# Dilated attention with its values made in a stage of their own: six projection blocks per head instead of nine, queries in reversed order

## The chip, the cores and the metric

The kernel runs on one core of one Trainium2 chip. The metric is the device time of one execution in microseconds (us). Each kernel has several runs, of which the median is given, and one further execution that the hardware profiler recorded. All views of the profile below come from that one recorded execution.

The engines of a core work side by side and meet at semaphores: TensorE (PE; its loads of the stationary operand are listed apart as PEld), VectorE (DVE), ScalarE (ACT), GpSimd (POOL) and SyncE (SP), which here only issues DMAs. Each engine takes its own instructions strictly in the order in which they are written.

## The reference, cut to what matters

The model has a first block (forgetful attention, retention, memory attention) and a second block. The change is in the dilated attention of the second block: three groups of four heads; head j of all three groups is joined by the weights of their softmax denominators.

```python
DILATED_PATTERNS = ((128, 1), (512, 4), (2048, 16))     # window, dilation of a group
h = rms_norm(x, norm_mix_pre)
q, k, v, glu_in, gates = split(h @ w_in)                # 512 positions, 12 heads of 128
for g, (window, r) in enumerate(DILATED_PATTERNS):      # heads 4g .. 4g+3
    # query t sees the keys t - j*r, j = 0 .. window//r
    s = q @ k.T * Dh**-0.5 + bias[bucket(distance)]     # masked outside the window
    m = max(s); p = exp(s - m); l = sum(p)
    o = (p @ v) / l
w = l * exp(m - max over groups of m)                   # joined over the groups
a = sum(w * o) / sum(w)
y_a = a @ w_attn_out
c = silu(layer_norm(causal_conv(glu(glu_in), 31 taps))) # beside it
y_c = c @ conv_pw_w
mixed = sigmoid(gates_a) * y_a + sigmoid(gates_c) * y_c
```

## The kernel before

**Projections.** Activations lie with channels on the partitions and 512 positions along the row, as a high and a low part (`Hh`, `Hl`). Weights come in blocks of 512 KB from DRAM (`wraw`, issued by SP, line 515), ACT rounds them to a high part (`whi`, helper `split`, line 755), POOL makes the low part (`wlo`, line 600), and PE multiplies them with the activations in 24 matmuls of 512 columns per block (`products`, lines 2190 to 2192: high by high, high by low, low by high). The blocks go round a ring of four places. The DMA of block n is issued when PE has finished block n-4; ACT's `split` call that stands at block b of its program handles block b+3, POOL's handles block b+2. So a weight block that lands late first blocks ACT, with all that stands behind the `split` in ACT's program.

**The dilated stage ("dil").** For each of the four heads j, nine blocks in the order of `DIL_BLOCKS`: q and k of group 0, of group 1, of group 2, then v of the three groups. DVE takes each result out of PSUM and scales it by the row norm: q to `dq`, k to `dk` in reversed order of positions (lines 1950, 1953), v to `dvT` (line 1956). For groups 1 and 2 the positions are read by residue mod 4. As the value operand must have positions on the partitions, PE turns `dvT` by four transposes per group (`d_values`, line 2646) and ACT copies the result to `dv` (`d_vtok`, line 1136): 12 times in all.

A head's softmax goes over two layouts: lay 0 (group 0, tiles of 128 consecutive positions) and lay 1 (groups 1 and 2, by residue). The steps are: `d_score(h, lay)` on PE; `d_soft` on DVE (bias and row maximum, line 1856); `d_exp` on ACT (line 1094); `d_store` and `d_load` on ACT's DMA queue (lines 1102 and 1108), which carry the row maxima and sums through a small DRAM buffer from one layout to the other; `d_diffs` on DVE; `d_weights_of` on ACT (line 1113); `d_weigh` on DVE; `d_norm` on ACT (line 1121, eight instructions, which signal after four and after eight); `d_turn` on PE (15 transposes, line 2616); `d_copy` on ACT (line 1128); `d_weigh_band` and `d_weigh_residues` on PE (lines 2627, 2637); `d_result` on ACT and DVE. The last head has a small matmul (`d_swap`) in place of the trip through DRAM.

**What lies beside it.** DVE computes the convolution of 31 taps for 8 chunks as 248 instructions (`taps`, line 1817), some behind each evacuation. POOL sums the chunks (line 696) and their squares (line 702), and PE forms mean and variance from the sums; ACT and DVE then normalise the chunks (`layer_norm`, lines 1147 to 1168 and 1918 to 1926) during the last head. The order on each engine is written out by hand: `d_stage(h, b)` is ACT's list for block b of head h, and the loops at the end of each engine's program are those of DVE and PE. Where PE stands at a block, the step that needs another engine's result is placed some blocks later.

## Time and profile before

| | |
|---|---|
| median of 3 runs | 1819.2 us (1818.88 to 1819.79) |
| the profiled execution, its own time | 1818.85 us |
| its span in the profile | 1817.2 us |
| PE busy | 1809.6 us (100% of the span) |
| PEld, DVE, ACT, POOL busy | 83%, 50%, 42%, 43% |
| "dil" stage | from about 1010 us to about 1242 us of the span |

The busy time of PE is the union of its matmuls, whose recorded ends overlap. How fast PE really goes is read from the distance between the starts of successive instructions in the timeline. "Idle before" in a row is the time for which the engine stood still before the instruction, and the name behind the arrow is what ended that.

### The profile page before, as it was taken

Reading aid. Unit: us, or ns where it says so; the run is one execution under the profiler, and the core shown is the slowest. Engines: PE = TensorE matmul, PEld = TensorE weight load, DVE = VectorE, ACT = ScalarE, POOL = GpSimd, SP = SyncE. Lnnn points to the kernel's source line nnn. Section 1 sums busy time; section 2 is a strip of 40 time slices with the busy share of each in tenths; the row PEclk is TensorE's granted clock in tenths of the full one; section 3 lists DMA queues with packets and bytes.
Section 4 is the critical chain, followed back from the end, with each engine's and each line's share of the span. In section 5 each row is a group of like instructions: output and inputs, shape, how many; then the busy total and the mean of one; then the engine's idle time right before and its main releaser. Section 6 shows DMA issues by size and latency. Waiting matters only on the chain.

```text
span 1817.2 us, 23583 instructions
## 1 busy us (share of the span) xinstructions
PE 1809.6 (100%) x8529; PEld 1500.7 (83%) x8529; DVE 916.1 (50%) x1583; ACT 759.7 (42%) x1228; POOL 786.6 (43%) x380
## 2 busy tenths in 40 slices
PE   9999999999999999999999999999999999999998
PEld 7888888888888777888888888888888888888887
DVE  6246566454210565544249989866333564544202
ACT  5344344443233565543343233257223474444213
POOL 3544443443444333443444543353444454444442
PEclk9999999999999999999999999999999999999999
DMA  5333333323333323332333443322333333333332
GB/s 175 100 93 83 92 81 93 111 82 105 93 93 115 93 81 93 98 100 81 103 93 93 113 89 83 81 82 69 94 102 94 93 93 93 92 103 105 95 102 93
DMA packets 285751, 173.99 MB, mean 96 GB/s; under 512 B 14800, under 2 KB 271208, under 8 KB 285664
## 3 DMA queue, kind: packets, MB, share of 16 engines
q1 hardware_dynamic: 275264, 164.70, 31.6%
q0 software_dynamic: 2496, 8.07, 1.5%
q10 hardware_dynamic: 7904, 0.06, 0.2%
q8 instruction: 55, 0.90, 0.2%
q14 instruction: 32, 0.26, 0.1%
HBM read 170.62 MB, written 2.19 MB: 95 GB/s over the span
## 4 chain that ended last, share of the span: by engine, by line
PE 99%; DVE 0%; ACT 0%; DMA 0%; issue 0%; DVEq 0%; ACTq 0%
PE proj L2190 23%; PE proj L2192 23%; PE proj L2191 23%; PE A L2508 1%; PE A L2510 1%; PE A L2509 1%; PE A L2871 1%; PE A L2873 1%; PE A L2872 1%; PE A L2348 1%; PE A L2446 1%; PE PV L2446 1%; PE proj L2510 1%; PE proj L2509 1%; PE proj L2508 1%; PE A L2438 1%
## 5 line engine op out<-in xcount | busy, mean ns | idle before, releaser
L600 POOL TENSOR_TENSOR wlo<-wraw,whi 128x1024 fp32r<-128x1024 f32 (+1 forms) x304 | 721.2, 2376 | 922.0 <-ACT whi L755 917.2
L755 ACT ACTIVATE whi<-wraw 128x1024 fp32r<-128x1024 f32 (+1 forms) x303 | 317.7, 1050 | 626.4 <-DMA wraw<-w_in 159.5
L2190 PE MATMUL proj<-Hh,whi 128*128 128x512 f32 x1424 | 562.8, 395 | 0.0
L2192 PE MATMUL proj<-Hh,wlo 128*128 128x512 f32 x1424 | 555.2, 390 | 0.0
L2191 PE MATMUL proj<-Hl,whi 128*128 128x512 f32 x1424 | 554.7, 390 | 0.0
L2192 PEld LDWEIGHTS proj<-Hh,wlo 128*128 128x128 f32 x1424 | 267.2, 188 | 56.7
L2190 PEld LDWEIGHTS proj<-Hh,whi 128*128 128x128 f32 x1424 | 267.5, 188 | 54.8 <-issue 0.7
L2191 PEld LDWEIGHTS proj<-Hl,whi 128*128 128x128 f32 x1424 | 267.6, 188 | 54.2 <-issue 0.7
L1817 DVE SCALAR_TENSOR_TENSOR A<-cin,dwT,A 128x512 f32<-128x512 f32 x232 | 175.1, 755 | 6.8
L2190 PE MATMUL proj<-Oh,whi 128*128 128x512 f32 x256 | 99.8, 390 | 0.0
L2191 PE MATMUL proj<-Ol,whi 128*128 128x512 f32 x256 | 99.6, 389 | 0.0
L2192 PE MATMUL proj<-Oh,wlo 128*128 128x512 f32 x256 | 99.6, 389 | 0.0
L1732 DVE TENSOR_TENSOR X<-X,proj 128x512 f32 (+1 forms) x16 | 11.0, 688 | 93.9 <-PE proj L2192 93.9
L2192 PEld LDWEIGHTS proj<-Oh,wlo 128*128 128x128 f32 x256 | 48.0, 188 | 10.1
L2190 PEld LDWEIGHTS proj<-Oh,whi 128*128 128x128 f32 x256 | 48.1, 188 | 9.8
L2191 PEld LDWEIGHTS proj<-Ol,whi 128*128 128x128 f32 x256 | 48.1, 188 | 9.8
L2126 DVE TENSOR_TENSOR uv<-proj,rms 128x512 f32<-128x512 f32 x21 | 14.5, 692 | 81.3 <-PE proj L2192 81.3
L2164 DVE TENSOR_TENSOR VT<-VT,gains 128x512 f32<-128x512 f32 x1 | 0.7, 700 | 101.2 <-ACT sq L1395 101.2
L858 ACT ACTIVATE ztanh<-z 128x512 f32<-128x512 f32 x20 | 12.6, 632 | 72.2 <-DVE z L1612 43.1
L1989 DVE TENSOR_TENSOR sq<-proj,rms 128x512 f32<-128x512 f32 x16 | 11.0, 690 | 54.0 <-PE proj L2192 54.0
L2508 PE MATMUL A<-whi,Hh 128*128 128x512 f32 x96 | 37.8, 394 | 0.0
L1586 DVE SCALAR_TENSOR_TENSOR ob<-PV,gate 128x512 f32<-128x512 f32 x20 | 13.8, 691 | 47.1 <-PE PV L2371 25.7
(553 smaller groups left out, 2948.8 us busy)
## 6 DMA issues: line engine op xcount, KB each, us to landing
wraw<-w_in SPq DMA_DIRECT2D x68, 512.0 KB, 3.8
wraw<-fox_w_in SPq DMA_DIRECT2D x56, 512.0 KB, 3.8
wraw<-ret_w_in SPq DMA_DIRECT2D x44, 512.0 KB, 3.8
wraw<-w_up SPq DMA_DIRECT2D x44, 512.0 KB, 3.8
wraw<-w_out SPq DMA_DIRECT2D x40, 512.0 KB, 4.0
wraw<-w_down SPq DMA_DIRECT2D x22, 512.0 KB, 3.6
wraw<-w_mem_kv SPq DMA_DIRECT2D x16, 512.0 KB, 3.9
wraw<-conv_pw_w SPq DMA_DIRECT2D x8, 512.0 KB, 4.0
```

The lines of the kernel that those rows point to most:

```text
L600: pool.tensor_tensor(wlo[s][:, 0:r, :], wraw[s][:, 0:r, :], whi[s][:, 0:r, :].bitcast(F32), ALU.subtract).then_inc(w_lo, 1)
L755: f(whi[s][:, 0:r, :], wraw[s][:, 0:r, :], ACT.Copy).then_inc(w_hi, 1)
L1817: ins = stt(conv_sum if tap < CONV - 1 else C[:, c, :], cin[:, c, tap:tap + S], dwT[:, c * CONV + tap:c * CONV + tap + 1], conv_sum, ALU.m ...
L2190: mm(dst, whi[s][:, c, :], xh, start=(first and c == 0), stop=False)
L2191: mm(dst, whi[s][:, c, :], xl, start=False, stop=False)
L2192: ins = mm(dst, wlo[s][:, c, :], xh, start=False, stop=(last and c == chunks - 1))
L2348: ins = pe.transpose(A[j][:, (i - j) * P:(i - j + 1) * P], probs[:, FOXAT[i] + j * P:FOXAT[i] + (j + 1) * P], ident[:])
L2438: ins = mm(ret_place(e, j), k[rows, j * P:(j + 1) * P], q[rows, j * P:S], start=True, stop=True)
L2446: ins = mm(ret_sum[e][:, j * P:S], values[:, r, j * P:(j + 1) * P], decayed[e][:, TRI[j]:TRI[j] + S - j * P], start=(j == 0), stop=(j == N ...
L2508: mm(y, Hh[:, x, at], high[:, c, :], start=(x == 0), stop=False)
L2509: mm(y, Hl[:, x, at], high[:, c, :], start=False, stop=False)
L2510: ins = mm(y, Hh[:, x, at], low[:, c, :], start=False, stop=(x == KC - 1))
```

## The change

- The values of all heads of a group are made by a new stage "vd" between "glu" and "dil". Its twelve weight blocks (four per group, each 2 x 128 rows by 512 columns, which is the values of four heads) are the moving operand, and 128 positions of `Hh` or `Hl` are the stationary one, so the result has positions on the partitions at once. Again 24 matmuls per block (`dil_values`, new lines 2635 to 2637). For groups 1 and 2 the stationary operand is read by residue, every fourth element of the row (`tokens_of`). ACT takes the tiles out of PSUM and applies the row norm as a scale per partition (`keep_dil`, new line 1186, 12 instructions).
- That scale per partition, `d_roots`, comes from eight matmuls of one column (new line 2607), four of them with `rms` read by residue, and one DVE instruction.
- `d_values`, `d_vtok` and the evacuation to `dvT` are gone; a head has six blocks. The steps of its softmax are spread anew over six blocks: `d_score(h, 1)`, its exp, its store and both loads move to the first two blocks of the next head, `d_turn` behind its fourth and the weighing behind its fifth.
- Queries are stored in reversed order instead of keys, the result is read reversed, and the bias table is mirrored.
- 84 taps of the convolution move to the new stage, and the sums, the layer norm and the last head's steps are placed anew.

```diff
-DIL_BLOCKS = ((0, 0), (0, 1), (1, 0), (1, 1), (2, 0), (2, 1), (0, 2), (1, 2), (2, 2))
-CHUNK_SUMS = (0, 5, 10, 15, 21, 26, 29)
+TAPS_GLU, TAPS_VALUES = (6, 5), 84
+TAPS_DIL = ((6, 6, 6, 6, 4, 6), (4, 4, 6, 8, 8, 5), (4, 4, 6, KC * CONV, 0, 0), (0, 0, 0, 0, 0, 0))
+DIL_BLOCKS = ((0, 0), (0, 1), (1, 0), (1, 1), (2, 0), (2, 1))
+CHUNK_SUMS = (0, 4, 8, 13, 18, 23, 27)
+SQUARE_SUMS = {29: (1, 2, 3), 30: (4, 5), 31: (6, 7)}
+        def tokens_of(x, spread, t):
+            return residues(x)[:, t, :] if spread else x[:, t * P:(t + 1) * P]
 # ACT
+            def keep_dil(group):
+                for j in range(NT):
+                    if j < NT - 1:
+                        act.wait_ge(v_summed[1], (NT - 1) * (GROUPS + group) + j + 1)
+                    else:
+                        act.wait_ge(w_used, PH["vd"].n(0, 4 * group + 3) + 1)
+                    f(dv[group][:, :, j * P:(j + 1) * P], value_banks[(NT * group + j) % 7][:]..., ACT.Identity,
+                      scale=d_roots[:, ...]).then_inc(v_kept[1], 1)
+            for b in range(PH["vd"].nb):
+                if b in (4, 8):
+                    keep_dil(b // 4 - 1)
+                split("vd", 0, b)
+            keep_dil(2)
             def d_stage(h, b):
+                if b == 0:
+                    split("dil", 0, nb)
+                    if h:
+                        d_load(h - 1, 1)
+                        d_exp(h - 1, 1)
+                        d_store(h - 1, 1)
+                if b == 1:
+                    split("dil", 0, nb)
+                    if h:
+                        d_load(h - 1, 0)
+                        d_weights_of(h - 1)
+                if b == 2:
+                    if h:
+                        d_norm(h - 1)
+                    split("dil", 0, nb)
+                    if last:
+                        layer_norm(5)
+                if b == 3:
+                    split("dil", 0, nb)
+                    if last:
+                        layer_norm(6)
+                if b == 4:
+                    if h:
+                        for x in range(4):
                             d_copy(h - 1, x, x)
+                    split("dil", 0, nb)
+                    if last:
+                        layer_norm(7)
+                    if h:
                         d_result(h - 1)
                     d_exp(h, 0)
                     if not last:
                         d_store(h, 0)
...
 # DVE
+                    n = TAPS_DIL[h][b]
+                    if b == 0 and h:
+                        taps(min(n, 1))
+                        d_soft(h - 1, 1)
+                        n = max(n - 1, 0)
+                    taps(n)
+                    if b == 1 and h:
+                        d_diffs(h - 1)
+                        d_weigh(h - 1)
+                    if h == last and b > 1:
+                        layer_norm(nb - 15)
+                    if b == 4:
+                        d_soft(h, 0)
+                        if h:
+                            d_result(h - 1)
 # PE
+                    if nb < 2:
+                        pe.wait_ge(v_kept[1], NT * GROUPS + 11 + nb)
+                    products("dil", 0, nb, nb, H)
+                    if b == 0 and h:
+                        d_score(h - 1, 1)
+                    if b == 3 and h:
+                        for x in range(4):
+                            d_turn(h - 1, x, x)
+                    if b == 4:
+                        if h:
                             d_weigh_band(h - 1)
-                            d_weigh_residues(h - 1, 0)
-                            d_turn(h - 1, 3, 0)
+                            d_weigh_residues(h - 1)
+                        d_score(h, 0)
-                    if b == 7:
-                        d_values(h, 0)
-                    if b == 8:
-                        d_values(h, 1)
+                    if h == JOINED - 1 and b == 1:
                         pe.wait_ge(c_sq_summed, KC - 1)
                         mm(A[3][:], mean_d[:], c_sq_sum[:], ...).then_inc(l_var, 1)
```

**PE, end of a value block.** Before, behind each of the twelve value blocks stand four transposes of the scaled values (`ident` is the identity):

```order
L2190 MATMUL proj<-Hh,whi 128x512
L2191 MATMUL proj<-Hl,whi 128x512
L2192 MATMUL proj<-Hh,wlo 128x512
L2646 MATMUL VT<-ident,dvT 128x128 x4
L2190 MATMUL proj<-Hh,whi 128x512
L2191 MATMUL proj<-Hl,whi 128x512
```

Now the value blocks end in the new stage and the first q block follows at once:

```order
L2635 MATMUL proj<-whi,Hh 128x512
L2636 MATMUL proj<-whi,Hl 128x512
L2637 MATMUL proj<-wlo,Hh 128x512
L2208 MATMUL proj<-Hh,whi 128x512
L2209 MATMUL proj<-Hl,whi 128x512
L2210 MATMUL proj<-Hh,wlo 128x512
```

The transposes have left PE's list, and nothing stands in their place.

**ACT, from the exp of lay 0 to the norm of a head.** Before, within one head (`whi<-wraw` are the weight splits, `128x8x1` is the store of lay 0, `128x2x4` that of lay 1):

```order
L1094 ACTIVATE dS,dstat<-dS,dstat 128x256 x3
L1102 DMA stat_scratch<-dstat 128x8x1
L755 ACTIVATE whi<-wraw 128x1024 x2
L1108 DMA dstat<-stat_scratch 128x2x4
L755 ACTIVATE whi<-wraw 128x1024
L1094 ACTIVATE dS,dstat<-dS,dstat 128x256 x4
L1102 DMA stat_scratch<-dstat 128x2x4
L1136 ACTIVATE dv<-VT 128x512
L1108 DMA dstat<-stat_scratch 128x8x1
L755 ACTIVATE whi<-wraw 128x1024
L1136 ACTIVATE dv<-VT 128x512
L1113 ACTIVATE dstat<-dstat 128x16
```

Now:

```order
L1106 ACTIVATE dS,dstat<-dS,dstat 128x128
L1114 DMA stat_scratch<-dstat 128x8x1
L767 ACTIVATE whi<-wraw 128x1024 x2
L1120 DMA dstat<-stat_scratch 128x2x4
L1106 ACTIVATE dS,dstat<-dS,dstat 128x256 x4
L1114 DMA stat_scratch<-dstat 128x2x4
L767 ACTIVATE whi<-wraw 128x1024
L1120 DMA dstat<-stat_scratch 128x8x1
L1125 ACTIVATE dstat<-dstat 128x16
L1133 ACTIVATE dS<-dS,dstat 128x256 x3
L1133 ACTIVATE dS<-dS,dstat 128x128
L1133 ACTIVATE dS<-dS,dstat 128x256 x4
```

Between the store of lay 0 and the exp of lay 1 stand two splits instead of three, and the load `128x2x4` comes ahead of that exp with no split between them.

**ACT, the copies of the turned weights of the third head (h = 2), during the last head.** Before, the copies (`dST<-A`) are done before any normalising:

```order
L755 ACTIVATE whi<-wraw 128x1024
L1128 ACTIVATE dST<-A 128x512
L1128 ACTIVATE dST<-A 128x384
L1128 ACTIVATE dST<-A 128x512
L755 ACTIVATE whi<-wraw 128x1024
L1128 ACTIVATE dST<-A 128x512
L1143 ACTIVATE squares<-C 128x512 x8
```

Now they stand behind two rounds of `layer_norm` (`C<-C,vec` and `squares<-C` for chunks 0 to 3), of which this is the end:

```order
L767 ACTIVATE whi<-wraw 128x1024
L1166 ACTIVATE C<-C,vec 128x512
L1169 ACTIVATE squares<-C 128x512
L1166 ACTIVATE C<-C,vec 128x512
L1169 ACTIVATE squares<-C 128x512
L1176 ACTIVATE Ch<-C 128x512 x2
L1140 ACTIVATE dST<-A 128x512
L1140 ACTIVATE dST<-A 128x384
```

What moved is the place of the copies against the layer norm; their number is the same.

## Rows read from the trace of the kernel before

**Rows 1.** Waits of PE over the whole span: us in total, times, longest.
```profile
PE PV L2201 <- DVE mean_d L1418: 1.2, 1, 1.2
```
**Rows 2.** Busy time by stretch: PE, PEld, DVE, ACT, POOL, PEclk, DMA share, GB/s.
```profile
1100.00:1200.00 100.00, 100.00 (x503) 84.40 (x502) 90.52 (x154) 36.90 (x72) 42.88 (x20) 1.00 0.34 85
```
**Rows 3.** Timeline of PE: start, duration (us), line, operation, tiles.
```profile
1040.60 0.39 PE L2190 MATMUL proj<-Hh,whi 128*128 128x512 f32 x1
1046.04 0.39 PE L2190 MATMUL proj<-Hh,whi 128*128 128x512 f32 x1
...
1091.05 1.68 PE L2608 MATMUL A<-dk,dq 128*128 128x128 f32 x8
1092.38 0.59 PE L2190 MATMUL proj<-Hh,whi 128*128 128x512 f32 x1
...
1122.10 0.60 PE L2646 MATMUL VT<-ident,dvT 128*128 128x128 f32 x4
1128.03 0.60 PE L2646 MATMUL VT<-ident,dvT 128*128 128x128 f32 x4
```
**Rows 4.** One line's instructions: the one-column matmuls of the earlier norm.
```profile
L2560 PE MATMUL VT<-mean_d,rms x8: 165/250/250, 520.5 to 521.2; 128*128 128x1 f32 x8
```
**Rows 5.** DMA issues by tile, KB each, median us to landing (page; then short windows).
```profile
wraw<-w_in SPq DMA_DIRECT2D x68, 512.0 KB, 3.8
...
stat_scratch<-dstat ACTq DMA_DIRECT2D x1, 4.0 KB, 11.4
...
stat_scratch<-dstat ACTq DMA_DIRECT2D x1, 4.0 KB, 2.7
...
dstat<-stat_scratch ACTq DMA_DIRECT2D x1, 4.0 KB, 2.7
```
**Rows 6.** Groups by line, ACT and POOL, 1190 to 1240 us: busy, mean ns.
```profile
L755 ACT ACTIVATE whi<-wraw 128x1024 fp32r<-128x1024 f32 x7 | 7.4, 1051 | 7.7 <-DMA wraw<-w_in 7.6
L1158 ACT ACTIVATE C<-C,vec 128x512 f32<-128x512 f32 x5 | 4.1, 810 | 3.9 <-DVE C L1922 3.9
L1161 ACT ACTIVATE squares<-C 128x512 f32<-128x512 f32 x4 | 2.5, 632 | 0.1
L762 ACT ACT_TABLE_LOAD x1 | 1.3, 1283 | 0.0
L1136 ACT ACTIVATE dv<-VT 128x512 f32<-128x512 f32 x2 | 1.2, 576 | 0.0
...
L600 POOL TENSOR_TENSOR wlo<-wraw,whi 128x1024 fp32r<-128x1024 f32 x7 | 16.7, 2397 | 21.6 <-ACT whi L755 21.6
L702 POOL TENSOR_TENSOR c_sq_sum<-c_sq_sum,squares 128x512 f32<-128x512 f32 x6 | 7.7, 1291 | 0.6
```
**Rows 7.** Timeline of ACT around the store of lay 0, heads 1 and 0.
```profile
1097.16 0.37 ACTq L1102 DMA_DIRECT2D stat_scratch<-dstat  x1
1111.40 1.06 ACT L755 ACTIVATE whi<-wraw 128x1024 fp32r<-128x1024 f32 x1 [14.27 <-DMA wraw<-w_in]
...
1053.22 1.06 ACT L755 ACTIVATE whi<-wraw 128x1024 fp32r<-128x1024 f32 x1 [13.96 <-DMA wraw<-w_in]
```
**Rows 8.** Timeline, DVE and ACT of head 1: taps, statistics, norm.
```profile
1117.95 4.71 DVE L1817 SCALAR_TENSOR_TENSOR A<-cin,dwT,A 128x512 f32<-128x512 f32 x6
1123.82 0.72 DVE L1889 TENSOR_TENSOR dstat<-dstat 128x8 f32<-128x8 f32 x1
...
1124.85 0.22 ACT L1113 ACTIVATE dstat<-dstat 128x16 f32<-128x16 f32 x1 [1.51 <-DVE dstat L1892]
1127.09 3.20 ACT L1121 ACTIVATE dS<-dS,dstat 128x128 f32<-128x128 f32 x8 [2.03 <-DVE dstat L1907]
```
**Rows 9.** Timeline of DVE: evacuation in plain order, then by residue.
```profile
1130.01 0.68 DVE L1950 SCALAR_TENSOR_TENSOR dq<-proj,rms 128x512 f32<-128x512 f32 x1
1140.82 1.10 DVE L1950 SCALAR_TENSOR_TENSOR dq<-proj,rms 128x512 f32<-128x512 f32 x1 [0.25 <-PE proj L2192]
```
**Rows 10.** Groups by line, DVE, 1000 to 1240 us: busy, mean ns of one.
```profile
L1856 DVE CUSTOM_DVE_ANT_0 dS<-A,btab 128x256 f32<-128x256 f32 (+1 forms) x32 | 11.4, 403 | 2.4 <-PE A L2608 1.9 <-PE A L2604 0.3
```

More of the change, by code:

```diff
@@ L229, in build @@
             C = sb("C", [P, KC, S], F32, two)
+            with ExitStack() as values_of_heads:
+                dv = [sb(f"dv{g}", [P, JOINED, S], F32, values_of_heads) for g in range(2)]
             Ah = sb("Ah", [P, JOINED, S], F32R, two)
@@ L703, in sum_square @@
                                    ALU.add).then_inc(c_sq_summed, 1)
-            for b in range(9 * JOINED):
-                split("dil", 0, b)
+            for b in range(PH["vd"].nb + PH["dil"].nb):
+                if b < PH["vd"].nb:
+                    split("vd", 0, b)
+                else:
+                    split("dil", 0, b - PH["vd"].nb)
                 if b in CHUNK_SUMS:
@@ L1239, in _ @@
             split("mix", 0, 0)
-            d_vtok(last, 2)
             mix_tanh(0, 0)
+            d_exp(last, 1)
             layer_norm(9)
+            split("mix", 0, 1)
             mix_tanh(0, 1)
-            for x in range(4):
-                d_copy(last, x, LAST_TURNED[x])
-            split("mix", 0, 1)
+            d_weights_of(last)
+            d_norm(last)
             split("mix", 0, 2)
             mix_tanh(1, 0)
-            d_result(last)
+            for x in range(4):
+                d_copy(last, x, x)
             split("mix", 0, 3)
             mix_tanh(1, 1)
+            d_result(last)
             split("mix", 1, 0)
@@ L1940, in _ @@
             for h in range(JOINED):
-                for b in range(9):
+                for b in range(PER_HEAD):
                     g, c = DIL_BLOCKS[b]
-                    nb = 9 * h + b
+                    nb = PER_HEAD * h + b
                     arrived("dil", 0, nb)
@@ L2586, in _ @@
                 products("glu", 1, b, b, H, par=1, bank=(A[2], PV)[b], free=0)
+            pe.wait_ge(evac, PH["glu"].g(0, 0) + 1)
+            for n in range(2 * NT):
+                ins = mm(VT[:, n:n + 1], tokens_of(rms, n // NT, n % NT), mean_d[:, 0:1], start=True, stop=True)
+            ins.then_inc(v_spread[1], 1)
             with pe.Fori(1, KC // 2) as h:
```

258 lines of the change are left out of this document (109 added, 149 removed).

## The prediction

> **What bounds the kernel now.** I read the busy times of the page first, then PE's waits, then the stretch from 1000 to 1240 us by engine, then the timeline of PE there, and last those of ACT, DVE and the DMAs. PE is busy for the whole span, and its longest wait for another engine is 1.2 us, at the very start [rows 1]. In the stretch of the change PE is 100% busy at a granted clock of 1.00, that is 2.4 GHz, while DVE stands at 91% and ACT at 37% [rows 2]. So the time is the sum of what PE issues. An instruction taken from PE gains its whole issue time, and a wait put on PE costs its whole length, for nothing downstream has slack to give it back. A projection block takes 1046.04 - 1040.60 = 5.44 us: the two rows are 24 matmuls apart [rows 3].
>
> **What PE loses and gains.** From one group of four transposes to the next are 1128.03 - 1122.10 = 5.93 us with one block between them [rows 3], so four transposes cost 0.49 us. Twelve groups go: -5.9 us. The values themselves cost what they cost before, 12 blocks of 24 matmuls of 512 columns. The eight matmuls of one column are new. The earlier ones of this kind appear in eight records for four matmuls, from 520.5 to 521.2 us [rows 4], 0.10 to 0.11 us a record; sixteen records: +1.8 us. Scores, turns and weighing keep their number. PE's own work falls by 4.1 us. Against the profiled execution's 1818.85 us that is 1814.8 us, if PE never waits. The median of the runs is 0.35 us above that execution.
>
> DVE loses twelve evacuations of 0.7 to 1.1 us and gains none; ACT's twelve copies of 0.58 us [rows 6] stay twelve. Neither is on PE's path by its amount. What matters is the order.
>
> **The stationary operand by residue.** 192 matmuls of the new stage load every fourth element of `Hh` or `Hl`. No row of before has such a load. The nearest is DVE's: an evacuation read by residue takes 1.10 us instead of 0.68 [rows 9], a factor of 1.6. Four transposes in 0.49 us show that a load of 128 columns, with its short matmul, is repeated every 0.12 us. By DVE's factor that would be 0.19 us, by twice 0.24, by four times 0.49; a matmul of 512 columns covers 0.227 (5.44 / 24). The lower end is 0 us, the upper (0.49 - 0.227) x 192 = 50 us. I take 0, the value nearest to the DVE rows, and keep the upper end as a rival.
>
> The Trainium skill, Advanced Engine Details and Errata, section Memory Cachelines, says that SBUF needs two hits on a 16-byte line to run at full rate, which a read of every fourth float32 never has; it gives no price. By that rule the load is slower, and the sum changes only if it exceeds the 0.227 us. The DVE rows agree in sign, but they read PSUM as well.
>
> **The waits that come.** Before, a head's steps were spread over nine blocks (49 us); now they have six (33 us) and a chain with two trips through DRAM. I follow it with a clock t that starts when PE ends a block; scores of lay 0 take 1.4 us (1092.38 - 1091.05, [rows 3]), those of lay 1 sixteen records of 0.11 = 1.8, 15 transposes 1.7, the weighing 30 records = 3.3.
>
> What decides is the store of lay 0. In before it lands 11.4 us after its issue, where that of lay 1 lands after 2.7 [rows 5], and the weight DMA that is issued beside it lets ACT go on only 14.0 to 14.3 us after the store instead of after 3.8 [rows 5, 7]. The order of before hid both, since PE has no such wait [rows 1]. The Trainium skill, DMA: Bandwidth & Descriptors, in its first table, says that transfers under 512 B are done by read-modify-write. The 4-byte pieces of this store are such; that page would leave the store of lay 1 slow too, which the rows contradict. The price used here is that of the rows.
>
> *First q block.* `keep_dil(2)` stands behind the split of the last value block. That block's DMA lands 3.8 after PE's start on it, the split takes 1.06, three copies 3 x 0.58 [rows 5, 6]: 6.7 us, and PE is done after 5.4. Wait: 1.3 us (bounds 0 and 2).
>
> *Turn of head 0.* t = 0 at the end of its fifth block. DVE: evacuation 1.0, four taps 3.1 (4.71 / 6 each, [rows 8]), row maxima 4 x 0.40 [rows 10] and a small one: 5.9. ACT's exp, estimated at 2.0 from the norm's 0.4 per instruction and the read of each sum [rows 8], ends at 7.9; store at 8. PE ends the sixth block at 1.4 + 5.44 = 6.8; so a weight DMA is issued 1.2 us before the store and meets it. If it is held up, its split comes at 8 + 14 = 22 and ends at 23. Behind this split ACT has the exp of lay 1: 25; its store lands at 28, the load at 30.9. DVE: differences, ACT's small exp, factor: 2.2 to 2.3 us (1123.82 to 1127.09 less two taps of 0.8, [rows 8], with the hand-overs): 33.2. The norm's first half is done at 34.8, the second at 36.5. PE ends the fourth block of the next head at 6.8 + 5.44 + 1.8 + 3 x 5.44 = 30.4, plus 0.9 for the low part of the late block (23 + 2.4 = 25.4 against 24.5, rounded): 31.3. Seven transposes wait until 34.8 (3.5 us), eight more until 36.5 (0.9). Sum 5.3. If the DMA slips through ahead of the store, the exp starts 3.5 us earlier and 1.9 remain. I take the middle, 3.6.
>
> *Turn of head 1.* DVE waited for head 0's statistics and now has 22 taps (17 us) and three evacuations before the maxima: they come 12 us after PE's fifth block (33.2 + 17.3 + 3.0 + 1.8 = 55.3 on head 0's clock, where that block ends at 36.5 + 0.9 + 5.44 = 42.8). Exp and store at 14.2, landing at 25.6. `d_load(h, 1)` waits for that landing and stands ahead of the exp of lay 1: 27.7, store lands 30.5, load 33.2, factor 35.5, norm 37.1 and 38.8. PE: 3.3 + 1.4, two blocks, 1.8, three blocks = 33.7. Wait 3.5 + 0.9 = 4.4.
>
> *Variance of the convolution.* In head 2 no taps are left; the store goes at 7.9, before PE ends its sixth block at 3.3 + 1.4 + 0.5 + 5.44 = 10.7. The weight DMA issued then lands at 22, split 23, POOL's low part 25.4; behind it stand the last two sums of squares, 2 x 1.3 [rows 6]: 28. PE wants them after two blocks and 1.8: 23.4. Wait 4.6. What is queued behind it on PE is everything; ACT and DVE wait for the variance too.
>
> *Weighing of head 2.* u = 0 where PE wanted the variance; it has it at 5.1. ACT: exp of lay 1 behind the late split, 1.5; store and load to 7; factor 9.2; norm 12.5; split 13.5; table load 1.28, Ln and Exp 1.2: 16; then chunks 0 and 1, 2 x 1.44 [rows 6], another table load and 0.7 of DVE: 20.9; split 21.9; chunks 2 and 3: 24.7; two roundings 1.2; four copies 2.3: 28.2. PE: 5.1, two blocks, the turn, one block: 23.1. Wait 5.1.
>
> Sum: 1.3 + 3.6 + 4.4 + 4.6 + 5.1 = 19.0. Time: 1818.85 - 4.1 + 19.0 = 1833.8, against the median 1834.
>
> **Rivals.**
> 1. *The store of lay 0 holds nothing up, or only for 8 us.* Here the store and the weight DMAs meet at other distances than before. Then the turns of heads 0 and 1 come in time, the variance waits 0.8 and the weighing 5.1 (its queue on ACT doesn't need the store): 7.2 with the first wait. 1814.8 + 7.2 + 0.35 = 1822. Against it: both heads shown were held up alike, by 14.0 and 14.3 us [rows 7].
> 2. *Faster: PE doesn't wait.* The place is ACT in the last head: if ACT reaches the copies of `dST` within 18 us of the variance instead of 23, and the store is harmless, the transposes are gained whole: 1815, 4 us faster. It decides from 5 us less on that chain. For it: ACT is busy for 37% only. Against it: it is a chain of single steps, and none is shorter than its row.
> 3. *Slow strided loads.* 1834 + 50 x a part; at four times the load time 1884, at two and a half (0.29 us) 1846.
> 4. *A wait that grows.* A DMA held up once more, or the store landing 12 us late twice: 24 to 28 us of waits, 1840 to 1843.
>
> **Numbers.** Forecast 0.62 (waits of 12 to 23 us); rival 1 0.17, rival 2 0.07, rival 3 0.06, rival 4 0.08. A measurement of this kernel tells 0.2%, 3.6 us, from no change, so no change is 1815.6 to 1822.8: rival 2 and the luckiest part of rival 1 split there. Faster 0.07, same 0.10, slower 0.83. The forecast's own range is 1826 to 1838; with rivals 1 and 4 it is 1821 to 1843.
>
> **What would show it.** After: PE's waits would list `dS` or the norm behind ACT before the turns of the first two heads (4 to 5 us each), a wait for POOL's `c_sq_sum` (4 to 5) and for ACT's `dST` before the weighing of the third head (5); ACT would stand 10 us or more for `wraw` after each store of lay 0. The value matmuls of groups 1 and 2 would start every 0.227 us; a longer distance makes rival 3 right. If PE's list of waits is as short as now, the forecast is wrong at its core.

## The result: 1839.1 us, slower, and the profile after

| | before | after |
|---|---|---|
| median of the runs, us | 1819.2 (1818.4 to 1819.8) | 1839.1 (1838.7 to 1841.2) |
| profiled execution, us | 1818.85 | 1840.74 |
| its span, us | 1817.2 | 1839.1 |
| mean granted clock of TensorE | 1.00 | 0.996 |

The ratio is 1.0113 [1.0101, 1.0124]. By the medians the change costs 19.9 us, by the two profiled spans 21.9 us. The forecast was 1834, its own range 1826 to 1838, and with its rivals 1821 to 1843. The measured median lies 1.1 us above the own range and inside the wide one.

The waits of PE after the change, over the whole span (us in total, times, longest). In before the last of these lines was the whole list down to 1.2 us [rows 1]:

```profile
PE A L2673 <- ACT dS L1133: 7.7, 5, 2.8
PE A L2726 <- POOL c_sq_sum L711: 4.5, 1, 4.5
PE proj L2208 <- ACT dv L1186: 1.4, 1, 1.4
PE PV L2683 <- ACT dST L1140: 1.4, 1, 1.4
PE PV L2219 <- DVE mean_d L1444: 1.2, 1, 1.2
```

The four new lines add up to 15.0 us. The wait for `dv` stands ahead of the first query block, at 1083.87 us. The timeline of PE says where the others stand (start, duration, line, operation, then in brackets the idle time before it and what ended it):

```profile
1144.65 0.99 PE L2673 MATMUL A<-ident,dS 128*128 128x128 f32 x7 [2.74 <-ACT dS L1133]
1146.25 1.11 PE L2673 MATMUL A<-ident,dS 128*128 128x128 f32 x4 [0.61 <-ACT dS L1133]
...
1191.01 2.71 PE L2673 MATMUL A<-ident,dS 128*128 128x128 f32 x11 [2.79 <-ACT dS L1133]
...
1228.17 2.07 PE L2726 MATMUL A<-c_sq_sum,mean_d 128*128 128x512 f32 x2 [4.53 <-POOL c_sq_sum L711]
...
1230.47 0.63 PE L2209 MATMUL proj<-Hl,whi 128*128 128x512 f32 x1
1230.90 0.63 PE L2210 MATMUL proj<-Hh,wlo 128*128 128x512 f32 x1
...
1250.28 1.83 PE L2683 MATMUL PV<-dST,dv 128*128 128x128 f32 x14 [1.41 <-ACT dST L1140]
...
1281.80 0.98 PE L2673 MATMUL A<-ident,dS 128*128 128x128 f32 x7 [0.90 <-ACT dS L1133]
1283.40 0.66 PE L2673 MATMUL A<-ident,dS 128*128 128x128 f32 x4 [0.61 <-ACT dS L1133]
```

From the top: the turns of heads 0 and 1, the variance, the weighing of head 2, and the turn of the last head. The rows behind the variance hold a second cost. A matmul of 512 columns starts 0.43 us after the one before it (1230.47, 1230.90), where elsewhere in these traces it is 0.23. The busy time by stretch shows the same as a lower granted clock (PEclk, the third value from the right; 0.66 to 0.72 over a stretch is a mixture of 1.2 and 2.4 GHz):

```profile
1144.00:1150.00 6.00, 4.74 (x21) 4.12 (x22) 5.82 (x8) 6.00 (x13) 2.78 (x2) 0.72 0.21 64
1190.00:1196.00 6.00, 4.99 (x24) 4.39 (x25) 5.82 (x9) 6.00 (x13) 2.41 (x1) 0.72 0.25 75
1228.00:1233.00 5.00, 4.83 (x13) 3.22 (x14) 1.19 (x8) 1.09 (x4) 2.42 (x2) 0.66 0.11 1
1250.00:1256.00 6.00, 5.72 (x42) 5.43 (x43) 6.00 (x7) 5.48 (x9) 2.74 (x1) 1.00 0.29 87
```

The clock is down behind the waits of 2.74, 2.79 and 4.53 us, and stays at 1.00 behind that of 1.41. Each of the three stretches lost 1.7 us by it (0.28 x 6, 0.28 x 6, 0.34 x 5): 5.1 us. In before it was 1.00 from 1100 to 1200 us [rows 2].

Why the two turns waited shows on ACT's timeline in head 0 (ACTq is ACT's issue of a DMA; layer 0 and layer 1 are the two layouts, lay 0 and lay 1). It answers to [rows 7] and [rows 8]:

```profile
1119.39 0.40 ACTq L1114 DMA_DIRECT2D stat_scratch<-dstat  x1
...
1128.38 1.06 ACT L767 ACTIVATE whi<-wraw 128x1024 fp32r<-128x1024 f32 x1 [7.43 <-DMA wraw<-w_in]
1131.66 0.37 ACTq L1120 DMA_DIRECT2D dstat<-stat_scratch  x1
1132.08 0.51 ACT L1106 ACTIVATE dS<-dS,dstat 128x256 f32<-128x256 f32 x1 [2.63 <-DMA stat_scratch<-dstat]
...
1137.67 0.37 ACTq L1120 DMA_DIRECT2D dstat<-stat_scratch  x1
...
1143.00 3.20 ACT L1133 ACTIVATE dS<-dS,dstat 128x256 f32<-128x256 f32 x8 [0.95 <-DVE dstat L1937]
```

The store of layer 0 leaves at 1119.39. The weight block that travels beside it lets ACT go on at 1128.38, 9.0 us after it. The load of layer 1's statistics, which needs the store's landing, can go only at 1131.66, 12.3 us after the store; the exponentials of layer 1 stand behind that load, though nothing in them needs it. The rest is a chain of single steps up to 1143.00, and PE's turn starts 1.65 us after that. The hold-up of the weight block is not the same in every head: ACT gets it 9.0 us after the store in head 0, 3.9 us in head 1 (1166.53 to 1170.40) and 14.3 us in head 2 (1207.72 to 1221.99). The load's wait for the store's landing is 12.3 us in head 0 and 11.1 us in head 1 (1166.53 to 1177.66).

The value blocks themselves answer to [rows 3]: the starts of four of the twelve, the first two in plain order, the others by residue.

```profile
1015.40 0.39 PE L2635 MATMUL A<-whi,Hh 128*128 128x512 f32 x1
1020.84 0.39 PE L2635 MATMUL A<-whi,Hh 128*128 128x512 f32 x1
...
1037.17 0.40 PE L2635 MATMUL proj<-whi,Hh 128*128 128x512 f32 x1
1042.81 0.40 PE L2635 MATMUL proj<-whi,Hh 128*128 128x512 f32 x1
```

A block takes 5.44 us in plain order and 5.64 by residue.

### The profile page after: what moved, and what is told of

Same layout as the page of the kernel before. It is cut to its first block, busy times and chain, and to the rows that moved or that the text cites. A ratio compares the mean times of both kernels' runs of the same rounds, so it can differ in the third digit from the quotient of the medians.

```text
span 1839.1 us, 23466 instructions
## 1 busy us (share of the span) xinstructions
PE 1816.8 (99%) x8497; PEld 1512.8 (82%) x8497; DVE 909.3 (49%) x1572; ACT 759.0 (41%) x1228; POOL 786.9 (43%) x380
## 4 chain that ended last, share of the span: by engine, by line
PE 91%; DMA 3%; DVE 3%; ACT 2%; issue 1%; ACTq 0%; DVEq 0%; SPq 0%
PE proj L2208 20%; PE proj L2210 20%; PE proj L2209 20%; DMA stat_scratch<-dstat 2%; DVE A L1843 1%; PE A L2526 1%; PE A L2527 1%; PE A L2528 1%; PE A L2905 1%; PE A L2907 1%; PE A L2906 1%; DMA wraw<-w_in 1%; PE A L2366 1%; PE A L2464 1%; PE PV L2464 1%; PE proj L2527 1%
## 5 line engine op out<-in xcount | busy, mean ns | idle before, releaser
L2208 PE MATMUL proj<-Hh,whi 128*128 128x512 f32 x1328 | 525.5, 396 | 1.4 <-ACT dv L1186 1.4
L2210 PE MATMUL proj<-Hh,wlo 128*128 128x512 f32 x1328 | 518.5, 390 | 0.0
L2209 PE MATMUL proj<-Hl,whi 128*128 128x512 f32 x1328 | 518.1, 390 | 0.0
L2208 PEld LDWEIGHTS proj<-Hh,whi 128*128 128x128 f32 x1328 | 250.5, 189 | 53.9 <-ACT dv L1186 1.7
L2210 PEld LDWEIGHTS proj<-Hh,wlo 128*128 128x128 f32 x1328 | 249.8, 188 | 53.0
L2209 PEld LDWEIGHTS proj<-Hl,whi 128*128 128x128 f32 x1328 | 250.4, 189 | 51.0 <-issue 1.0
L2000 DVE TENSOR_TENSOR sq<-proj,rms 128x512 f32<-128x512 f32 x16 | 11.1, 691 | 55.6 <-PE proj L2210 55.5
L2528 PE MATMUL A<-wlo,Hh 128*128 128x512 f32 x96 | 37.4, 389 | 0.0
```

Source lines behind the costliest of these rows:

```text
L2208: mm(dst, whi[s][:, c, :], xh, start=(first and c == 0), stop=False)
L2209: mm(dst, whi[s][:, c, :], xl, start=False, stop=False)
L2210: ins = mm(dst, wlo[s][:, c, :], xh, start=False, stop=(last and c == chunks - 1))
L2528: ins = mm(y, Hh[:, x, at], low[:, c, :], start=False, stop=(x == KC - 1))
```

## The experiments

Every run is compared with runs of before on the same chip (medians 1819.1 to 1819.4); after stands at a ratio of 1.0113.

| run | edit | median, us | ratio to before |
|---|---|---|---|
| e1_contiguous | after, stationaries in plain order | 1835.0 | 1.0085 [1.0068, 1.0102] |
| e2_spread | after, one-column matmuls spread | 1836.6 | 1.0094 [1.0077, 1.0111] |
| e3_store16 | after, short store | 1829.0 | 1.0049 [1.0033, 1.0066] |
| e4_no_turns | before, 12 transposes instead of 48 | 1815.8 | 0.9981 [0.9971, 0.9990] |
| e5_squares | after, squares summed earlier | 1838.2 | 1.0104 [1.0088, 1.0119] |
| b_store16 | before, short store | 1819.5 | 1.0000 [0.9991, 1.0010] |
| e6_mended | after, four mendings | 1821.9 | 1.0015 [1.0006, 1.0024] |
| e7_late_squares | before, squares summed later | 1826.7 | 1.0042 [1.0026, 1.0057] |
| e8_order | after, ACT's list reordered | 1835.3 | 1.0087 [1.0072, 1.0102] |
| e9_all | after, reordered and mended | 1828.7 | 1.0050 [1.0036, 1.0064] |
| e10_all_plain | e9_all in plain order | 1826.7 | 1.0042 [1.0029, 1.0056] |
| e11_native | after, mended, gathering load | 1819.9 | 1.0005 [0.9996, 1.0014] |

### Is it the store? (e3_store16, and b_store16 in before)

```diff
-                to = (stats_by_tile, stats_by_residue)[lay](h, lay)
+                to = stats_by_residue(h, lay)
```

> The changed kernel, with the store of lay 0 written in the pattern of the store of lay 1 (pieces of 16 bytes instead of 4; the statistics then reach other rows, so the weights between groups are mixed up, with the same instructions). Theory of the prediction: that store is what holds up the weight DMAs and the exp of lay 1; without it the waits before the turns of heads 0 and 1 (3.4 and 2.8 us) and most of the wait for the sums of squares (4.5, down to 0 to 1) go, and with them the stretches of lower clock behind them (about 1.3 us each): 12 to 14 us less, 1825 to 1827 us. Rival (rival 1 of the prediction read the other way: the order on ACT alone makes the waits): at most 2 us less, 1837 us or more.

> The kernel before with the layer-0 maxima stored in pieces of 16 bytes (the order of layer 1) in place of 4; the output is then wrong in how the two layers are weighed. My theory: TensorE waited for nothing in this stage before the change, so a shorter store gives nothing: 1819.2 us, within 2 us. Rival: the long store also slows the weight loads and other work of the kernel before, and the store's 10 us are worth 2 us or more there as well: 1817 us or less.

In after this takes 10.2 us away; in before it changes nothing (1819.5 against 1819.2). The waits of PE that are left in e3_store16:

```profile
PE PV L2683 <- ACT dST L1140: 3.0, 1, 3.0
PE PV L2700 <- DVE swap_in L1899: 1.5, 1, 1.5
PE proj L2208 <- ACT dv L1186: 1.5, 1, 1.5
...
PE A L2726 <- POOL c_sq_sum L711: 1.0, 1, 1.0
```

No wait for `dS` is left, and that for `c_sq_sum` shrank from 4.5 to 1.0. So all waits of the turns of heads 0 and 1, and most of the variance's, come from the 4-byte store. It was as long in before and cost nothing there, since PE did not need what hung on it. Two waits grew in its place, 3.0 for `dST` and 1.5 for `swap_in`: of the 11.2 us of waits that went, 3.1 came back. The 1.5 us is that of the last head, which has no trip through DRAM: it stood at its turn in after and stands at its swap here. With the short store ACT gets the weight block of head 0 3.3 us after the store (1119.59), and not 9.0:

```profile
1122.89 1.06 ACT L767 ACTIVATE whi<-wraw 128x1024 fp32r<-128x1024 f32 x1 [1.74 <-DMA wraw<-w_in]
```

### Is it the store's length or ACT's order? (e8_order)

```diff
-                act.wait_ge(d_stored, 16 * (2 * h + (2 if lay == 0 else 1)))
+                act.wait_ge(d_stored, 16 * (2 * h + 2))
 ...
-                    split("dil", 0, nb)
-                    if h:
-                        d_load(h - 1, 1)
-                        d_exp(h - 1, 1)
-                        d_store(h - 1, 1)
+                    if h:
+                        d_exp(h - 1, 1)
+                        d_store(h - 1, 1)
+                    split("dil", 0, nb)
 ...
+                        d_load(h - 1, 1)
                         d_load(h - 1, 0)
```

> The changed kernel with ScalarE's list alone rewritten for heads 0 to 2: the exponentials and the store of layer 1 come ahead of the weight block they stood behind, and both loads of statistics come after both stores, one block later; the store of layer 0 keeps its 4-byte pieces, and the output stays the reference's. My theory: in the changed kernel the exponentials of layer 1 stood behind a load that waited for the long store (1131.66), while their maxima were ready at 1126.9. Both stores are then out by about 1129 and landed by 1133, the loads by 1137 to 1138, and the weights are multiplied in from about 1139 instead of 1143.0: the waits for dS (7.7 us) go, with some 3 us of lower clock behind them, and 2 to 4 us come back as waits for dST and the sums of squares, since TensorE is then early there: 1839.1 - 7.7 - 3 + 3 = 1831 us, 1829 to 1834. Rival: the 4-byte store's own length is what counts (layer 1's store and the weights' transfers queue behind it whatever the order), so that the loads land within 1 us of where they did: 1837 to 1839 us with waits for dS of 5 us or more.

Between the two: 1835.3. Both loads now wait for both stores. The exponentials of layer 1 came 5.4 us earlier (1132.08 to 1126.66), but the last load only 3 us (1137.67 to 1134.69). ACT's timeline in e8_order:

```profile
1119.09 0.40 ACTq L1114 DMA_DIRECT2D stat_scratch<-dstat  x1
...
1126.66 0.51 ACT L1106 ACTIVATE dS<-dS,dstat 128x256 f32<-128x256 f32 x1 [6.01 <-DVE dstat L1891]
...
1128.77 0.37 ACTq L1114 DMA_DIRECT2D stat_scratch<-dstat  x1
...
1134.69 0.89 ACTq L1120 DMA_DIRECT2D dstat<-stat_scratch  x2
```

The two stores are landed together only at 1134.69, 15.6 us after the first was issued and 5.9 us after the second, which by itself takes 2.7 [rows 5]. Of the 7.7 us of waits for `dS` 5.5 stay. The order alone gives 3.8 us, the short store alone 10.2: the store's length is the larger part.

### Is the variance's wait a cost of its own? (e5_squares)

```diff
-SQUARE_SUMS = {29: (1, 2, 3), 30: (4, 5), 31: (6, 7)}
+SQUARE_SUMS = {29: (1, 2, 3), 30: (4, 5, 6, 7)}
```

> The changed kernel with the last two sums of squares made one weight block earlier on GpSimd (blocks 29 and 30 in place of 29, 30 and 31). My theory: TensorE's wait for c_sq_sum (4.53 us) goes, and with it the lower granted clock behind it (0.66 over 5 us, worth 1.7 us); 0.5 to 2 us of it come back at the weighing of head 2, whose copies of dST do not move. Time 1839.1 - 4.5 - 1.7 + 1.5 = 1834.4 us, 1833 to 1836. Rival: ScalarE, and not GpSimd, sets the pace there, so that the wait moves in full to the weighing of head 2: 1838 to 1840 us, with a wait for dST of 5 to 6 us.

The rival was right in the time; the wait for `dST` is longer than its 5 to 6 us. The 4.5 us wait went, and this row of PE's waits in e5_squares takes its place, where after had 1.4:

```profile
PE PV L2683 <- ACT dST L1140: 7.3, 1, 7.3
```

1838.2 us is 0.9 us below the median of after, and the two ratios' intervals overlap. The waits of the changed stage still add up to 15.0 us (7.3, 4.9, 1.5 and 1.3), and the lower clock behind two of them took 6.8 us (3.4 each), where in after it took 5.1. The weighing of head 2 waits for ACT, whose layer norm stands ahead of the copies of `dST`. They are done 26.4 us after PE stood at the variance, in after 26.6; PE had only arrived 6.1 us earlier (19.1 us instead of 25.2). Four waits in one stage are not four costs.

### Does the clock fall because PE waited? (e7_late_squares, an edit of before)

```diff
-SQUARE_SUMS = {30: (1, 2, 3), 31: (4, 5), 32: (6, 7)}
+SQUARE_SUMS = {30: (1, 2, 3), 31: (4, 5), 33: (6, 7)}
```

> The kernel before with its last two sums of squares moved behind a weight block that is two later (blocks 30, 31 and 33 in place of 30, 31 and 32), nothing else: a wait of TensorE is put into a kernel that has none there. By the rows of the kernel before GpSimd finishes that weight block at 1224.6 us and the sums 2.7 us later, where TensorE stands at 1222.0: a wait of 5.3 us. My theory: the granted clock falls behind it as it did in the changed kernel (0.66 over 5 us behind a wait of 4.5), so that the time grows by the wait and another 1.5 to 2.5 us: 1819.2 + 7.3 = 1826.5 us. Rival: the low clock in the changed kernel had another cause (the values' stage or the store): the time grows by the wait alone, 1824.5 us, and the clock stays 1.00 behind it.

PE's timeline in e7_late_squares:

```profile
1226.80 2.07 PE L2694 MATMUL A<-c_sq_sum,mean_d 128*128 128x512 f32 x2 [4.81 <-POOL c_sq_sum L702]
...
1229.10 0.63 PE L2191 MATMUL proj<-Hl,whi 128*128 128x512 f32 x1
1229.53 0.52 PE L2192 MATMUL proj<-Hh,wlo 128*128 128x512 f32 x1
1229.89 0.39 PE L2190 MATMUL proj<-Hh,whi 128*128 128x512 f32 x1
```

In before the same fourth matmul of the block starts 1.56 us after the one for `c_sq_sum` (1222.02 to 1223.58), here 3.09 us (1226.80 to 1229.89). So a wait of 4.8 us costs 1.5 us more in lower clock, in a kernel that has neither the values' stage nor the new order. The sum, 6.3, is what the spans show (1823.2 less 1817.2 is 6.0); the medians give 7.4 [4.7, 10.4 by the ratio's interval]. The rival, the wait alone, is refuted by the rows more than by the medians.

The traces of the other runs give the spread. By one less the granted clock, times the length of the stretch, 1.7 or 1.8 us were lost behind twelve of the fifteen waits from 2.5 to 7.3 us, and 3.4 behind the other three (3.90 in e1_contiguous, 2.80 and 7.28 in e5_squares). Behind 1.93 us in e9_all 1.7 were lost, behind 1.86 and 2.31 in e2_spread and 2.41 in e9_all nothing, and behind waits up to 1.75 nothing. So the length of a wait alone does not say what follows it.

### What do the strided loads cost? (e1_contiguous)

```diff
-... tokens_of(Hh[:, x, :], group, j), tokens_of(Hl[:, x, :], group, j)
+... tokens_of(Hh[:, x, :], 0, j), tokens_of(Hl[:, x, :], 0, j)
```

> The changed kernel, with the stationary operands of the value blocks of groups 1 and 2 read in plain order instead of by residue (the values are then those of other positions; the instructions are the same in number and size). The trace of the changed kernel shows the eight blocks of groups 1 and 2 at 5.64 us each and the four of group 0 at 5.44, and their weight loads at 309 ns instead of 188. Theory that the stride costs: all twelve blocks 5.44 us, 8 x 0.2 = 1.6 us less than the changed kernel, 1837.5 us. Rival, that the 0.2 us comes from what runs beside these blocks: 1839.1 us, blocks still 5.64.

One line's weight loads by tile (duration in ns, least, median, most), here in after, where 24 of this tile's 32 loads are by residue:

```profile
L2635 PEld LDWEIGHTS proj<-whi,Hh x32: 187/309/311, 1017.2 to 1081.4; 128*128 128x128 f32 x32
```

and the same line in e1_contiguous:

```profile
L2635 PEld LDWEIGHTS proj<-whi,Hh x32: 187/188/188, 1015.3 to 1077.9; 128*128 128x128 f32 x32
```

A load of every fourth element takes 309 ns instead of 188, a factor of 1.64, and the block gets 0.20 us longer (all twelve take 5.44 us in e1_contiguous); eight blocks: 1.6 us. The medians fell by 4.1 us, and the two ratios' intervals just touch. The two profiled spans differ by 3.5 us, and the starts of PE's matmuls divide them: 0.6 us lie ahead of everything that the change touches, 1.3 behind the one-column matmuls, where the clock did not fall this time (below), and 1.6 in the eight blocks. e10_all_plain, the same edit on e9_all, gives 2.0 by the medians and again 1.6 in the blocks.

### What are the transposes and the one-column matmuls worth? (e4_no_turns, an edit of before, and e2_spread)

```diff
-                for j in range(NT):
+                for j in range(1):
                     ins = pe.transpose(VT[:, j * P:(j + 1) * P], dvT[:, j * P:(j + 1) * P], ident[:])
```

> The kernel before, with one transpose instead of four in each of the twelve groups that turn the values (three quarters of the values are then stale). The first term of the sum: 36 transposes at 0.12 us go, 4.4 us less, 1814.8 us, PE without a new wait. Rival, that PE's time is set by something else and a taken transpose only makes a gap: 1819.2 us.

3.5 us [1.8, 5.3 by the interval] for three quarters of the transposes, where 4.4 were worked out. The starts in e4_no_turns say more than the medians:

```profile
1121.56 0.27 PE L2646 MATMUL VT<-ident,dvT 128*128 128x128 f32 x1
...
1127.15 0.27 PE L2646 MATMUL VT<-ident,dvT 128*128 128x128 f32 x1
```

From one group to the next are 5.59 us, where before has 5.93 [rows 3] and a block alone takes 5.44. Three transposes are worth 0.34 us, the fourth 0.15, and the four 0.49. The 36 that went are worth 4.1 us; 0.8 of it came back at 1467.92, where PE now waits 0.61 us for `whi`, a wait that before does not have. So the 5.9 us for all 48 stand.

```diff
-            for n in range(2 * NT):
+            def d_spread(n):
 ...
+            products("glu", 1, 1, 1, H, par=1, bank=PV, free=0, each=d_spread)
```

> The changed kernel, with the eight one-column matmuls that turn the row norm put one by one ahead of the eight chunks of the second block of glu turn 1, instead of in one bunch behind it. In the changed kernel the bunch takes 2.7 us and the granted clock falls to 0.91 and 0.92 in the two stretches of 10 us around it; 3.9 us in all from the last matmul before to full pace again. Theory that the bunch lowers the clock: the clock stays at 1.00 there and the 16 records cost 16 x 0.11 = 1.8 us, so 2.1 us less, 1837.0 us. Rival, that these matmuls cost 2.7 us wherever they stand: 1838 to 1839.1 us.

1836.6 against 1839.1, with overlapping intervals: undecided by the medians. In after's profile the sixteen records lie from 945.97 to 948.64: 2.67 us, 0.17 each. Spread, they stand in pairs ahead of three matmuls of 512 columns. Two chunks with `rms` in plain order start so, and then two by residue:

```profile
940.15 0.28 PE L2609 MATMUL VT<-mean_d,rms 128*128 128x1 f32 x2
...
941.07 0.28 PE L2609 MATMUL VT<-mean_d,rms 128*128 128x1 f32 x2
...
945.93 0.40 PE L2609 MATMUL VT<-mean_d,rms 128*128 128x1 f32 x2
...
946.98 0.40 PE L2609 MATMUL VT<-mean_d,rms 128*128 128x1 f32 x2
```

A chunk alone takes 5.44 / 8 = 0.68 us. With a plain pair it takes 0.92, so a record costs 0.12 us, near the 0.11 of [rows 4]; with a pair by residue 1.05, 0.18 each. The whole block lasts from 940.15 to 948.01, 2.4 us longer than 5.44. So spreading saves 0.3 us of the matmuls themselves, and the theory's 1.8 was too low.

The rest is the clock. In after the granted clock of the stretches 940 to 950 and 950 to 960 us is 0.91 and 0.92. But e1_contiguous, which has the same bunch, shows this:

```profile
940.00:950.00 10.00, 10.00 (x49) 8.74 (x48) 9.43 (x13) 1.82 (x3) 4.66 (x2) 1.00 0.37 105
950.00:960.00 10.00, 10.00 (x45) 8.26 (x44) 6.66 (x11) 3.25 (x3) 3.28 (x2) 1.00 0.18 52
```

The clock fell with this bunch in the profiles of after, e3_store16 and e8_order, and not in those of e1_contiguous and e5_squares, though the instructions up to there are the same. Why is open.

### Mended together (e6_mended, e9_all, e10_all_plain, e11_native)

> The changed kernel with four edits at once: layer-0 maxima stored in pieces of 16 bytes (which puts wrong numbers into the weighing of the layers), the sixteen one-column matmuls spread over the chunks of a gate block, the last sums of squares one block earlier, and ScalarE's copies of dST for head 2 ahead of the layer norm's chunks. My theory: the savings add up: -10.1 (store, measured), -2.6 (spread, measured), -1.0 (wait for c_sq_sum that was left) and -3.0 with 1.5 of clock behind it (wait for dST that was left): 1839.1 - 18.2 = 1821 us, 1819 to 1824. That is the kernel before within its uncertainty and no gain, since the strided loads (1.6), the first query block (1.5) and the swap (1.5) are left against the transposes (3.5 to 5.9). Rival: each wait that goes makes the next one longer, as TensorE is ahead of the other engines by then: 1826 to 1829 us.

1821.9, where the sum of single savings said 1821. The copies ahead of the norm are this edit, in the last head's fourth block:

```diff
                     split("dil", 0, nb)
                     if last:
+                        for x in range(4):
+                            d_copy(h - 1, x, x)
                         layer_norm(6)
```

> The changed kernel with ScalarE's list as in e8_order, the one-column matmuls spread over the chunks, the last sums of squares one block earlier, the copies of dST for head 2 ahead of the layer norm, and the last head's second swap and its turns two chunks later each; nothing is left out of the computation. My theory: e6_mended (1821.9, which had the short store) shows what is left without these waits; with the order in place of the short store the waits for dS are gone as well, and the swap's wait (1.6 us) goes: 1820 to 1823 us, that is the kernel before or 0.1% to 0.2% above. What holds it there is the strided load (1.6 us) and the first query block's wait (1.4 us). Rival: the long store keeps delaying the weights' transfers, which the other mendings had nothing to do with: 1825 to 1830 us.

> e9_all with the stationary operands of the second and third group of the values read in plain order instead of by residue, so that the values of these groups stand at wrong positions; everything else as in e9_all. My theory: the strided loads cost 1.6 us in all (8 blocks of 5.64 us in place of 5.44): 1.6 us less than e9_all. Rival: they cost more than the matmuls' spacing shows, by slowing other engines' reads of the same memory: 3 us or more less than e9_all.

The rival was right on e9_all: 1828.7. Without the short store the other mendings leave 4.7 us of waits for `dS` and 1.9 for `dST`. The step to e10_all_plain is 2.0 us, with intervals that overlap.

The last run keeps the computation whole and the store short: the statistics are written as they lie, and gathered when they are read.

```diff
-                to = (stats_by_tile, stats_by_residue)[lay](h, lay)
+                to = stats_by_residue(h, lay)
 ...
-                of = (stats_by_tile, stats_by_residue)[lay](h, 1 - lay)
-                act.dma_start(dstat[:, 16 * lay + 8:16 * lay + 16], of, ...).then_inc(d_came, 16)
+                if lay == 0:
+                    act.dma_start(dstat[:, 8:16], stats_by_tile(h, 1), ...).then_inc(d_came, 16)
+                else:
+                    for k in range(2):
+                        of = bass.AP(s_dram.tensor, h * 4 * S + k * S, [[1, NT], [4 * NT, P // NT], [NT, NT]])
+                        act.dma_start(dstat[:, 24 + 4 * k:28 + 4 * k], of, ...).then_inc(d_came, 16)
```

> The changed kernel with the four mendings that the runs so far point to, and a short store that keeps the computation whole: layer 0's maxima and sums are stored as they lie, in pieces of 16 bytes, and the loads for layer 1 gather them in pieces of 4 bytes (two loads in place of one); the one-column matmuls are spread, the sums of squares are one block earlier, the copies of dST for head 2 come ahead of the layer norm, and the last head's second swap and turns come two chunks later. Nothing is left out of the computation. My theory: it is the writing of 4-byte pieces to memory that is slow (11 to 15 us), not their reading (3.7 us in the changed kernel): the loads land in 2 to 5 us, no wait for dS is left, and with the swap's 1.6 us gone from the 1821.9 us of e6_mended the time is 1820.3 us, 1819 to 1822: the kernel before within its uncertainty. Rival: the gathering load is as slow as the scattering store was, the waits for dS come back: 1826 to 1829 us, as in e9_all.

1819.9, a ratio of 1.0005 [0.9996, 1.0014]: no different from before. The gathering loads, and the landing of all its stores and loads, by the rows of the tile `stat_scratch`:

```profile
L1124 ACTq DMA_DIRECT2D dstat<-stat_scratch x6: 547/1044/1424, 1121.3 to 1204.3; - x6
...
DMA to landing us min/median/max: 1.5/2.0/3.3
```

None needs more than 3.3 us, the gathering loads of 4-byte pieces included. What PE still waits for in the changed stage:

```profile
PE proj L2214 <- ACT dv L1190: 1.3, 1, 1.3
...
PE PV L2694 <- ACT dST L1144: 0.5, 1, 0.5
```

The swap of the last head adds 0.2 us.

No version with the whole computation is faster than before. That fits the sum: 5.9 us for the transposes, against 1.6 for the strided loads, 2.4 for the spread one-column matmuls, and 2.0 of waits, leaves +0.1 us, where 0.6 was measured, [-0.7, 2.5] by the ratio's interval.

## Why the prediction was right, and where it was not

**What bounds the kernel.** Right. In before PE is the sum of what it issues. In e7_late_squares a wait put on it cost its whole length and more. An instruction taken away gave its whole issue time, but in e4_no_turns 0.8 of 4.1 us came back as a wait that before does not have.

**What PE loses and gains.** -5.9 for the transposes is borne out by the starts in e4_no_turns. The one-column matmuls were put at 0.11 us each, by rows that read `rms` in plain order; half of the new ones read it by residue. The sixteen took 2.67 us in after (945.97 to 948.64). Where the clock falls behind them, seven matmuls take 3.0 us instead of 1.6 (948.64 to 951.66). The term of +1.8 measured 2.7, or 4.1 with the clock.

**The stationary by residue.** The term was 0, it measured 1.6 us. DVE's factor of 1.6 was right (309 to 188 ns), and the 0.19 us worked out from it is near the 0.18 of a one-column matmul by residue in e2_spread. That it would hide wholly behind 0.227 was the wrong half: a matmul starts every 0.235 us (5.64 / 24), 0.008 more than in plain order. The recorded length of a load is not what has to fit: 0.31 - 0.227 on 192 matmuls would be 16 us. Why 0.008 is left over no run shows. The Trainium skill, Advanced Engine Details and Errata, section Memory Cachelines, says that a line needs at least two hits; the trace agrees with it in sign, 309 against 188 ns. No run here, with a stride of two say, shows that this is the cause. Rival 3's sign, matmuls further apart than 0.227, came, but at 1.6 us of its up to 50.

**The waits.** Predicted and measured, in us:

| place | predicted | measured | what ran otherwise |
|---|---|---|---|
| First q block | 1.3 | 1.4 | |
| Turn of head 0 | 3.6 | 3.35 | weights held up 9 us, not 14; exponentials of layer 1 held up by the landing instead |
| Turn of head 1 | 4.4 | 2.8 | the chain through the landing as reckoned; PE 0.4 us later, and no second wait of 0.9, as the turns ran at the lower clock |
| Variance | 4.6 | 4.5 | as reckoned, weights held up 14.3 us |
| Weighing of head 2 | 5.1 | 1.4 | PE 2.1 us later than reckoned, ACT 1.6 us earlier |
| Turn of the last head | none | 1.5 | not looked at |
| Sum | 19.0 | 15.0 | |

The mechanism, a slow store of layer 0 that the order of before had hidden, is shown by e3_store16 and b_store16. For head 0 the chain was right in its end and wrong in a link: I let the split be late by 14 us and the exponentials follow it, while the split was late by 9.0 and the load's wait, at 12.3, decided. That wait I had seen for head 1 only. The sign that ACT would stand 10 us or more for `wraw` after each store did not come: it stood 7.4, 2.4 and 8.6 us.

PE reached the weighing of head 2 at 25.2 us on the clock of that paragraph (1248.87, counted from 1223.64 where it wanted the variance) and not at 23.1. Most of that is the lower clock behind the variance's wait. ACT's copies ended at 26.6 instead of 28.2.

**The term that was missing.** The granted clock behind waits, 5.1 us in three stretches, is in no line of the prediction: every wait was priced at its length. How much later PE stands in after shows at two places, the last matmul ahead of the one-column ones and the first behind the dilated stage (before, after, before, after):

```profile
944.97 0.39 PE L2192 MATMUL PV<-Hh,wlo 128*128 128x512 f32 x1
945.74 0.39 PE L2210 MATMUL PV<-Hh,wlo 128*128 128x512 f32 x1
...
1269.82 0.39 PE L2190 MATMUL proj<-Ch,whi 128*128 128x512 f32 x1
1291.72 0.48 PE L2208 MATMUL proj<-Ch,whi 128*128 128x512 f32 x1
```

PE is 0.8 us late before the change begins and 21.9 behind it, so the change costs 21.1 us here. The measured terms are -5.9 + 4.1 + 1.6 + 15.0 + 5.1 = 19.9 us. The missing 1.2 fits how a wait is counted: idle time runs from the recorded end of a matmul, 0.39 us after its start, where without a wait the next one starts 0.23 after it. At eight places that is an estimated 1.3 us. That the terms alone give the 19.9 us of the medians is chance.

Term by term the forecast was 4.0 us too high in the waits, and too low by 5.1 in the clock, 2.3 in the one-column matmuls with their clock, 1.6 in the strided loads and 1.2 in the counting of waits. That is 6.2 us too low in all, and the time came out as near as it did only because the waits erred the other way. That part is luck.

**The rivals.** Rival 1's condition, a harmless store, is made in e3_store16. Its waits are 7.0 us, where the rival had 7.2; its time is 1829.0 and not 1822, by the terms that are too low in PE's own work (3.9 us with the clock behind the one-column matmuls) and the clock behind the wait of 3.0 us (0.72 from 1236 to 1242 us, 1.7). Rival 2 (PE never waits, 1815) is not reached even in e11_native, because of the first query block, the strided loads and the one-column matmuls. Rival 4 did not come: its waits were 24 to 28 us, and though its 1840 to 1843 is nearly the time measured, they were 15.0.

## What to carry to other kernels

On a kernel whose TensorE never waits, price a new wait at its length plus the lower clock behind it: 1.5 to 1.8 us for most waits of 2.5 us and more here, 3.4 for three of them, nothing for waits up to 1.75. A slow transfer that costs nothing in one order is a debt: list each before shortening the stage that hides it. Where a layout has to be changed on the way through DRAM, write the pieces as they lie and gather on the read, and look for the next waiter before taking a wait away.

## What was not expected of the hardware

- Writing 4 KB to DRAM in 4-byte pieces takes 11 to 12 us and can hold the neighbours up: ACT gets the weight block beside it 9.0, 3.9 and 14.3 us after the store in the three heads, and a store of 16-byte pieces issued behind it is landed only 5.9 us after its issue. Reading 4-byte pieces of the same 4 KB lands within 3.3 us, and writes of 16-byte pieces are as quick there. The Trainium skill, DMA: Bandwidth & Descriptors, in its first table, puts everything under 512 B into one class; here both 4 and 16 bytes are in it, and only the 4-byte write is slow.
- A weight load of every fourth float32 takes 309 ns instead of 188, and 0.20 us a block of 24 matmuls are not hidden. With its matmul of one column such a load costs 0.18 us instead of 0.12 (e2_spread).
- The granted clock behind a bunch of sixteen one-column matmuls fell (0.91 in after) in three profiles and stayed at 1.00 in two others of the same instructions.
